# Dense blocks of a two-model fp32 kernel: the weight's high part meets high and low activations in one 512-column product

## The reference

```
swiglu(h) = (silu(h @ w_gate) * (h @ w_up)) @ w_down      # w_gate, w_up: 1024 x F, w_down: F x 1024
F = 2816 in the four of the first network, 3584 in the dense one of the second
```

## Time and profile before

| | value |
|---|---|
| median of 3 executions | 2753.35 us (2750.55 to 2759.77) |
| profiled execution, first to last instruction (span) | 2747.2 us |
| the profiled execution's own device time | not listed apart; the median is 6.2 us above its span |
| TensorE matmul / weight load busy | 2600.3 us (95%) / 2379.0 us (87%) |
| VectorE / ScalarE / GpSimd busy | 2165.5 us (79%) / 1483.6 us (54%) / 947.8 us (34%) |
| DMA | 670.58 MB, mean 244 GB/s |
| granted TensorE clock, mean | 0.971 |

### The profile page before, as it was taken

How to read it: one execution, slowest core, us unless ns; L and a number is a source line. 1 busy time by engine, 2 the same in 40 slices (tenths; PEclk the granted TensorE clock), 3 DMA queues, 4 the chain that set the end, 5 groups by cost and what they waited for, 6 DMA issues and landing times. The chain is left out here.

```text
span 2747.2 us, 47482 instructions
## 1 busy us (share of the span) xinstructions
PE 2600.3 (95%) x17802; PEld 2379.0 (87%) x17802; DVE 2165.5 (79%) x2488; ACT 1483.6 (54%) x1930; POOL 947.8 (34%) x586
## 2 busy tenths in 40 slices
PE   8999899999998998888998978999999999999997
PEld 7999699999897998658998747999999999999986
DVE  5667666766787676987855997898989898989888
ACT  4337543443434334424334515777777777777765
POOL 6990089688789992126900130000000000000000
PEclk9999999999999998999999988999999999999999
DMA  8664267566566653324553415999999999999985
GB/s 309 252 237 148 103 241 256 202 250 254 191 241 229 220 183 134 115 105 164 183 184 138 164 63 192 343 350 333 352 335 349 338 347 343 347 345 346 340 320 216
DMA packets 129209, 670.58 MB, mean 244 GB/s; under 512 B 14672, under 2 KB 14992, under 8 KB 80064
## 3 DMA queue, kind: packets, MB, share of 16 engines
q1 hardware_dynamic: 111024, 604.72, 59.9%
q0 software_dynamic: 18064, 64.21, 6.9%
HBM read 667.82 MB, written 1.05 MB: 243 GB/s over the span
## 5 line engine op out<-in xcount | busy, mean ns | idle before, releaser
L1721 PE MATMUL work<-xT_hi,wh_gu 128*128 128x256 f32 x2088 | 593.9, 284 | 21.6 <-DVE xT_lo L985 12.0
L1722 PE MATMUL work<-xT_lo,wh_gu 128*128 128x256 f32 x2088 | 592.3, 284 | 0.0
L1723 PE MATMUL work<-xT_hi,wl_gu 128*128 128x256 f32 x2088 | 591.7, 283 | 0.0
L1721 PE MATMUL work<-wh_gu,mixT_hi 128*128 128x256 f32 x1792 | 507.5, 283 | 2.8 <-DVE wl_gu L1439 1.5
L1722 PE MATMUL work<-wl_gu,mixT_hi 128*128 128x256 f32 x1792 | 505.8, 282 | 0.0
L1723 PE MATMUL work<-wh_gu,mixT_lo 128*128 128x256 f32 x1792 | 505.5, 282 | 0.0
L857 DVE TENSOR_TENSOR wl_gu<-raw_gu,wh_gu 128x2048 fp32r<-128x2048 f32 x158 | 392.3, 2483 | 72.0 <-ACT wh_gu L395 71.5
L1721 PEld LDWEIGHTS work<-xT_hi,wh_gu 128*128 128x128 f32 x2088 | 401.3, 192 | 30.1 <-issue 21.3
L1722 PEld LDWEIGHTS work<-xT_lo,wh_gu 128*128 128x128 f32 x2088 | 401.7, 192 | 4.8
L1723 PEld LDWEIGHTS work<-xT_hi,wl_gu 128*128 128x128 f32 x2088 | 401.5, 192 | 0.0
L862 DVE TENSOR_TENSOR wl_d<-raw_d,wh_d 128x1024 fp32r<-128x1024 f32 x157 | 250.2, 1594 | 189.6 <-ACT wh_d L402 189.5
(11 more groups left out here) (436 smaller groups left out, 4785.6 us busy)
## 6 DMA issues: line engine op xcount, KB each, us to landing
raw_gu<-in_w_gu SPq DMA_DIRECT2D x271, 1024.0 KB, 5.2
raw_d<-in_w_d SPq DMA_DIRECT2D x269, 512.0 KB, 5.4
scratch<-in_w_gu SPq DMA_DIRECT2D x112, 1024.0 KB, 7.2
scratch<-in_w_d SPq DMA_DIRECT2D x112, 512.0 KB, 7.8
scratch<-in_w_mod POOLq DMA_DIRECT2D x96, 512.0 KB, 3.7
scratch<-in_s_b POOLq DMA_DIRECT2D x16, 256.0 KB, 2.9
rows<-in_norm_post POOLq DMA_DIRECT2D x6, 512.0 KB, 4.4
rows<-in_ln_g POOLq DMA_DIRECT2D x4, 512.0 KB, 5.5
```

Source lines behind the costliest of these rows:

```text
L1721: pe.matmul(out_, w[0], m[0], start=start, stop=False)
L1722: pe.matmul(out_, w[0], m[1], start=False, stop=False)
L1723: return pe.matmul(out_, w[1], m[0], start=False, stop=stop)
```

## The change

The two activation tensors become two halves of one tensor, so that one moving operand can hold both. Per k-block and per half (gate, up) TensorE issues two matmuls where it issued three: the weight's high part against [x_high, x_low] in one product of 512 columns into a whole bank, and the weight's low part against x_high, 256 columns, added to the first half of that bank. Gate and up now take a bank each, and a unit two banks (0 and 1, or 2 and 3, by parity). The bank's second half holds high x low by itself, so the halves have to be added: VectorE does it for gate and up in one reduction (1024 elements in per partition, 512 out) into a new SBUF tile `GU`, behind `gu_used`, with a new semaphore `gu_sum`. ScalarE's silu waits for `gu_sum` and reads `GU`; VectorE's multiply reads the up part from `GU`. The other users of `XH` and `XL` are as they were, `down` too.

```diff
-        XH, XL = sb("xT_hi", [P, KD, S], F32R), sb("xT_lo", [P, KD, S], F32R)
+        XHL = sb("xT", [P, 2, KD, S], F32R)
+        XH, XL = XHL[:, 0], XHL[:, 1]
...
+        GU = [view(7168 + 512 * i, 512).rearrange("p (c s) -> p c s", c=2) for i in range(2)]
...
+        gu_sum = sem("gu_sum")
...
+        def gate_up_banks(n):
+
+            return PB[:, 2 * (n % 2):2 * (n % 2) + 2, :].rearrange("p c (part s) -> p c part s", part=2)
...
-            def ffn(n0, dyn, nf):
+            def ffn(n0, dyn, nf, f0):
 
                 def steps(at):
-                    for n in (n0, n0 + 1):
+                    for r in range(2):
+                        n = n0 + r
                         hi_gu(n + 1, at)
-                        ge(act, gu_used, n + 1, at)
-                        act.activation(SG[n % 2], PB[:, n % 2, 0:S], ACT.Silu).then_inc(silu_done, 1)
+                        ge(act, gu_sum, f0 + r + 1, at)
+                        act.activation(SG[n % 2], GU[n % 2][:, 0], ACT.Silu).then_inc(silu_done, 1)
                         hi_d(n + 1, at)
...
                     lo_gu(n + 1, dyn + j)
                     if late is not None:
                         residual(late)
+                    dve.wait_ge(gu_used, dyn + j + (n + 1))
+                    dve.reduce_sum(GU[k], gate_up_banks(n).rearrange("p c part s -> p c s part"),
+                                   AX.X).then_inc(gu_sum, 1)
                     dve.wait_ge(silu_done, fdyn + j + (f0 + r + 1))
-                    link(TT(HF[k], SG[k], PB[:, k, S:2 * S], ALU.mult))
+                    link(TT(HF[k], SG[k], GU[k][:, 1], ALU.mult))
...
             def gate_up(n, dyn=0):
                 ge(pe, gu_lo, n + 1, dyn)
-                gu_block(n, 0, PB[:, n % 2, 0:S], XH, XL)
-                gu_block(n, 1, PB[:, n % 2, S:2 * S], XH, XL).then_inc(gu_used, 1)
+                b, fresh[0] = fresh[0], None
+                for half in range(2):
+                    both = gate_up_banks(n)[:, half]
+                    for k in range(KD):
+                        if half == 0 and b is not None and k % 2 == 0:
+                            pe.wait_ge(xt_l, 4 * b + k // 2 + 1)
+                        pe.matmul(both, wh_gu[n % 2][:, half, k, :], XHL[:, :, k, :], start=k == 0, stop=False)
+                        last = pe.matmul(both[:, 0], wl_gu[n % 2][:, half, k, :], XH[:, k, :], start=False, stop=k == KD - 1)
+                last.then_inc(gu_used, 1)
```

More of the change, by code:

```diff
@@ L833, in _ @@
                 if kind == "ffn":
-                    ffn(START[b], 0, nf)
+                    ffn(START[b], 0, nf, FSTART[b])
                 elif kind == "ab":
```

## The result

| | before | after |
|---|---|---|
| time, median (us) | 2753.69 (4 runs, 2750.55 to 2759.77) | 2767.17 (4 runs, 2766.58 to 2773.39) |
| ratio, 95% interval | | 1.0053 (1.0035 to 1.0071) |
| profiled span (us) | 2747.2 | 2771.5 |

The change makes the kernel 13.5 us slower; the forecast was no change. A later comparison, e15, gave 2770.24 against 2751.79, ratio 1.0063 (1.0048 to 1.0078): 18.5 us. TensorE does what the change wants of it, and VectorE, in the units beside GpSimd, does not.

What follows compares the result with a forecast made beforehand. The prediction took TensorE's pace to bound the dense blocks. It summed -12.4 us (TensorE) + 6 (block ends) + 6 (units beside GpSimd) = -0.4 us, time 2753.0 us, range 2743 to 2771.

Steps and rivals of the forecast that it cites:

- TensorE's pace: In all 116 units, 16 wide products each save 6.7 ns by `down`'s pace: 12.4 us won.
- Rival 1: TensorE's saving is larger, its extra cost all per instruction: 24.1 us saved, time 2741 us; chance 0.17.
- The reduction: VectorE's new strided addition of 1024 PSUM elements per partition takes 1.21 us, between 0.7 and 2.29.
- Rival 3: VectorE's strided reduction takes 2.3 us, costing 39 us instead of 6, time about 2786 us; chance 0.07.
- No new wait for TensorE in a quiet unit, none for loads and banks: Quiet units: VectorE needs 6.5 of about 8.43 us; load slips of 1 us and bank reuse cost nothing.
- With 1.87 us more TensorE stands that long: 3 x 1.9 = 5.6: Ends of blocks 0, 2, 3: one `down` covers the chain, so TensorE waits; taken as 6 us, bounds 2 and 9.
- The same 1.87 us: VectorE's added time per unit: 1.21 us for the reduction plus 0.66 us around silu.
- No slack at all: End of block 0: VectorE's low part ended at 203.36 and TensorE went on at 203.50.
- I take 6 us for all of it: Units sharing with GpSimd in blocks 5 and 7: overshoot 6 us less about 2 in hand, plus multiply's contention; bounds 0 and 25.
- Blocks 0, 2, 3 can't win much more, since `mod_columns` waits for GpSimd: Ends of blocks 0, 2, 3: little more to win, as `mod_columns(0)` at 207.16 waited for GpSimd's sums.
- Rival 2: VectorE becomes the pacer beside GpSimd in blocks 0, 2, 3, 5 and early 7: 22 us, time 2769 us; chance 0.26.
- the forecast case: Whole kernel: gain and losses nearly cancel at -0.4 us, time 2753.0 us, own range 2745 to 2761; chance 0.48.

Runs made afterwards that it cites:

- e15: The changed kernel as it is, timed again beside the kernel before: 2770.24 us, ratio 1.0063.
- e11: The changed kernel without GpSimd's modulation and table arithmetic, the table's stand-in memset cut into 64 pieces: 2735.68 us, ratio 0.9936 to the kernel before.
- e12: The kernel before without GpSimd's modulation and table arithmetic, the table's stand-in memset in 64 pieces: 2750.44 us, ratio 0.9989 to the kernel before.
- e1: The changed kernel without the addition of the halves, silu and multiply reading the first halves from PSUM: 2763.65 us, ratio 1.0041 to the kernel before.
- e7: The changed kernel with the last two units of blocks 0, 2 and 3 in the old form: 2759.04 us, ratio 1.0037 to the kernel before.
- e10: As e9, and the units beside the table (block 5's last 10, block 7's first 14) in the old form: 2752.16 us, ratio 1.0003.
- e13: Changed form in 86 of 116 units, old form near GpSimd, three modulation terms per end of blocks 0, 2, 3 on VectorE: 2740.89 us, ratio 0.9962.
- e14: The kernel before, every unit in old form, with the same three modulation terms on VectorE as e13: 2749.39 us, ratio 0.999.
- e5: The changed kernel with two of GpSimd's 24 modulation terms in blocks 0, 2, 3 on VectorE after the last unit: 2767.33 us, ratio 1.0058.
- e9: The changed kernel with two modulation terms of blocks 0, 2, 3 on VectorE, each right behind an h_lo of the last two units: 2760.17 us, ratio 1.003.
- e8: The changed kernel with 18 more useless 512-column products on TensorE before the last down of blocks 0, 2 and 3: 2764.07 us, ratio 1.0049.
- e3: The changed kernel without GpSimd's modulation and table arithmetic, one long memset standing in for the table: 2749.74 us, ratio 0.9991 to the kernel before.

## Why the prediction was wrong, step by step

- **TensorE's pace**: right, a little small. Taken 6.7 ns a product, 12.4 us; the unit gives 127 / 16 = 7.9 ns, 14.7 us, confirmed by e11 against e12 (14.8). Rival 1's 24 us was not there.
- **The reduction**: right, 1.216 us (taken 1.21). Rival 3 out.
- **No new wait for TensorE in a quiet unit, none for loads and banks**: right; the quiet end of block 7 runs at 8.4 us a unit (101.60 us are 12.1 units) with VectorE at 5.9 us busy.
- **"With 1.87 us more TensorE stands that long: 3 x 1.9 = 5.6"**: this step failed. It took the 1.87 us as the whole price. As the kernel is, the price is 4 us of standing and 4.0 to 5.6 us later at the next `gate_up`, 14.8 for three, 8.8 more than taken. I had only added the new instructions to the old times, and not asked which GpSimd instruction the shifted chain would meet. The evidence was in the trace before: the weight's part of 3.37 us, where 1.22 is usual, was a GpSimd hit just behind the chain. This is the addition that it met:

```profile
204.57 2.38 POOL L1653 TENSOR_TENSOR scratch<-scratch 128x1024 f32<-128x1024 f32 x1
```

  The low part of h began at 202.93; moved by 1.87 us it begins at 204.80, inside that addition. The fall of the clock after 4 us of idling was not in the sum at all.
- **The same 1.87 us, as the length of the chain**: mis-sized as well. It is what VectorE has more to do and to wait for, but silu's 0.66 us were in the chain from `gate_up` to h before. With GpSimd quiet the chain grows by 1.10 us (e11, e12). "No slack at all" was read beside GpSimd, whose hits were in it: the wide low part took 3.83 us and the cast 0.76, where 2.29 and 0.29 are usual. Without them there are 0.96 us of slack, TensorE is done 0.13 us earlier in the new form, and the stall is 0.31 us. Both errors make the price of the reduction by itself too high; what makes the real one higher still is GpSimd.
- **"I take 6 us for all of it"**, the units beside the table: mis-sized. From first to last `gate_up` block 5 took 4.9 us more and should have saved 21 x 0.127 = 2.7, so its cost is 7.6; block 7, by the same sum (4.1 + 3.4), 7.5: 15.1 in place of 6. The forecast was 8.91 us a unit, waits included. Measured are 74.43 / 8 = 9.3, of them 8.77 busy and 0.53 idle, against 8.41 offered. Without the reduction's 1.22 and the wait the older instructions take 7.55 us a unit where before they took 7.04: they meet GpSimd more. The overshoot is so 0.9 us a unit in place of 0.48, and the 2 us in hand that I took off aren't seen.
- **Blocks 0, 2, 3 can't win more, since `mod_columns` waits for GpSimd**: right, and shown by e1, 6.14 us of waiting.
- **Rival 2** had the number (2769) and half of the place. Its units beside the table were right. Its slower units in blocks 0, 2 and 3 didn't come (8.406 us each); the loss there is at the ends.

With the measured sizes the sum is -14.7 + 14.8 + 15.1 = +15.2 us, and the timed differences are 13.5 and 18.5. That the time came to lie inside the stated range is the width of the range, not the mechanism: the forecast case said no change.

Shown is that GpSimd beside VectorE turns -15 into +13 to +18: with its arithmetic taken away the change wins 14.8 us (e11, e12); with the longer VectorE chain taken away from it, part of the loss goes at each of the two places (e7, e10), and with both taken care of the changed form wins 8.5 us (e13, e14). With GpSimd's last terms moved the 4 us stalls go (e5, and two of three ends in e9), though the times came out 7 to 15 us above what I expected. Open is how the price of an end divides between the standing and the clock behind it (e8), what the unprofiled executions of e1 lost, 10 us beyond the profiled one, and what the clock's course adds or takes: 6 us behind block 7 and 6 us in block 0 from one profile to another.

## What to carry to other kernels

When a change lengthens a chain on VectorE that shares its time with GpSimd, don't price it by its own microseconds: look at which GpSimd instruction each two-input SBUF instruction of the chain will then stand beside. If that is one with two SBUF inputs, or a long memset (e3), take the whole of it as the possible wait; and don't take the slack of a chain from a place where GpSimd has already stretched it. The price falls due where only one short stage covers the chain; a few units at the edges can carry much of the loss (e7), and leaving these in the old form keeps the gain of the rest. Place GpSimd's last work so that it is done a unit or two before such an edge.

## What the runs showed of the hardware

- VectorE's subtraction with two SBUF inputs stands still behind GpSimd's addition for all of it. Low part of h 0.42 to 2.52 us, ended 0.28 us after the addition, which had begun 0.10 us earlier; 26 of 26 that began in such an addition did so. A cast went from 0.29 to 6.69 us and ended 0.15 us after a GpSimd memset. The reverse too: GpSimd's multiply 2.85 to 4.76 us in the block 0 rows, with the weight's part running until 200.72.
- GpSimd's multiply, one SBUF tile by a column, is another matter: 15 wide subtractions began 0.12 to 0.14 us behind one and took their usual 2.28 us, and the multiply took 5.03 to 5.06 in place of 2.85. It isn't always so: in before four low parts of h begun 0.09 us behind a multiply took 1.30 us. One of the 15, from after:

```profile
96.29 5.05 POOL L1663 TENSOR_SCALAR scratch<-scratch,small 128x1024 f32<-128x1024 f32 x1
```

```profile
96.43 2.28 DVE L865 TENSOR_TENSOR wl_gu<-raw_gu,wh_gu 128x2048 fp32r<-128x2048 f32 x1
```

- The Trainium skill, SBUF — State Buffer, section Who interferes with whom, has it that a VectorE instruction with two SBUF inputs contends with a GpSimd instruction that reads SBUF, and that the order of issue decides which of the two blocks. The rows beside the addition agree. The 15 beside the multiply don't: there the later one went through. As an estimate from the addition's row, a 0.42 us instruction beside it can cost up to 2.34 us more, which the forecast's sum for the block ends left out.
- Instructions that read PSUM were spared: 116 reductions at 1208 to 1226 ns, beside GpSimd or not, and before the multiply with one operand in PSUM at 406 to 422 ns.
- A 512-column fp32r product and the 256-column one behind it take 8.406 - 2.79 = 5.61 us for 16 pairs, 351 ns each; three of 256 took 359.
- After 4.05 us of idling the granted clock was 0.50, the 1.2 GHz level, for the rest of the last down of block 0: 0.43 us a 512-column matmul, against 0.23. The stretch in the windows view (columns as above):

```profile
206.30:210.60 4.30, 4.30 (x10) 3.42 (x11) 2.20 (x2) 0.05 (x1) 0.00 (x0) 0.50 0.35 126
```
